# Accumulating eight projection blocks behind each norm by input chunk, and ordering the first loads to match

## The reference, cut to what matters

```python
cond = jax.nn.silu(c)
for l in range(DEPTH):
    mod = cond @ ada_w[l] + ada_b[l]                 # 6 x 1024 values: shift, scale, gate, twice
    sh1, sc1, g1, sh2, sc2, g2 = jnp.split(mod, 6, axis=-1)
    h = rmsnorm(x, norm1_g[l]) * (1.0 + sc1[:, None]) + sh1[:, None]
    x = x + g1[:, None] * token_mixer(h, positions, w_in[l], ...)   # proj = h @ w_in, 6656 columns
    h = rmsnorm(x, norm2_g[l]) * (1.0 + sc2[:, None]) + sh2[:, None]
    x = x + g2[:, None] * peer(h, peer_wq[l], ...)                  # q = h @ wq, 2048 columns
return rmsnorm(x, final_g)
```

## Time and profile before

| | |
|---|---|
| median of 3 runs | 2004.83 us (2003.58 to 2005.3) |
| span of the profiled execution, first to last instruction | 2001.2 us |
| median less span | 3.6 us |
| PE / PEld busy | 1945.8 / 1854.1 us |
| DVE / ACT / POOL busy | 1710.9 / 1240.9 / 441.9 us |
| mean granted clock of PE | 0.991 |
| moved by DMA | 480.52 MB, mean 240 GB/s |

### The profile page before, as it was taken

One profiled execution on the slowest core, in us unless ns is written; L12 is line 12 of the kernel. 1 busy time (PEld: TensorE's weight loads), 2 busy tenths in 40 slices (PEclk: granted clock), 3 DMA queues, 4 the chain that ended last, 5 costly groups with the idle time before them and its releaser, 6 DMA issues.

```text
span 2001.2 us, 39536 instructions
## 1 busy us (share of the span) xinstructions
PE 1945.8 (97%) x14478; PEld 1854.1 (93%) x14478; DVE 1710.9 (85%) x3168; ACT 1240.9 (62%) x2387; POOL 441.9 (22%) x312
## 2 busy tenths in 40 slices
PE   6999999999999999999989998999999999999998
PEld 6899899999999999999978898999999999999997
DVE  7876988999799888888788878899988888888887
ACT  3478545666888655555555775566668885555554
POOL 0000000000556433344100000000016543443440
PEclk7999999999999999999999999999999999999999
DMA  8764755666666799988767557555665558999884
GB/s 334 276 238 149 262 191 171 200 199 203 212 214 208 251 319 324 321 322 322 257 229 249 206 173 248 197 190 197 200 210 169 165 163 289 323 319 321 323 321 139
DMA packets 133554, 480.52 MB, mean 240 GB/s; under 512 B 16048, under 2 KB 16688, under 8 KB 132784
## 3 DMA queue, kind: packets, MB, share of 16 engines
q1 hardware_dynamic: 114992, 411.74, 60.6%
q0 software_dynamic: 18432, 67.12, 8.9%
HBM read 473.61 MB, written 1.57 MB: 237 GB/s over the span
## 4 chain that ended last, share of the span: by engine, by line
PE 87%; DVE 6%; ACT 3%; issue 2%; DMA 2%; SPq 0%; POOL 0%; DVEq 0%; ACTq 0%
PE ps L1777 20%; PE ps L1773 12%; PE ps L1474 11%; PE ps L1416 9%; PE ps L1412 8%; PE ps L1413 8%; PE ps L1478 6%; PE ps L1409 2%; PE ps L1746 2%; PE ps L1518 2%; ACT w_hi L564 2%; DVE w_lo L865 1%; DMA raw<-in_win 1%; PE ps L1464 1%; PE ps L1705 1%
## 5 line engine op out<-in xcount | busy, mean ns | idle before, releaser
L865 DVE TENSOR_TENSOR w_lo<-raw,w_hi 128x1024 fp32r<-128x1024 f32 x664 | 812.0, 1223 | 164.3 <-ACT w_hi L564 161.6
L564 ACT CAST w_hi<-raw 128x1024 fp32r<-128x1024 f32 x664 | 695.1, 1047 | 395.7 <-PE ps L1416 204.5
L1777 PE MATMUL ps<-p_both,w_hi 128*128 128x448 f32 x1952 | 440.1, 367 | 1.0 <-DVE p_both L1255 1.0
L1412 PE MATMUL ps<-h_both,w_hi 128*128 128x224 f32 (+1 forms) x1640 | 393.9, 282 | 2.5 <-ACT big L569 1.2
L1413 PE MATMUL ps<-h_both,w_hi 128*128 128x224 f32 (+1 forms) x1640 | 386.4, 278 | 0.0
L1777 PEld LDWEIGHTS ps<-p_both,w_hi 128*128 128x128 f32 x1952 | 349.3, 189 | 24.5 <-issue 1.3
L540 POOL TENSOR_SCALAR hot<-con,rt 128x128 f32<-128x128 f32 x168 | 198.1, 1190 | 640.0 <-DVE neg L1330 528.4
L1412 PEld LDWEIGHTS ps<-h_both,w_hi 128*128 128x128 f32 x1640 | 314.1, 192 | 5.5 <-issue 3.3
L1413 PEld LDWEIGHTS ps<-h_both,w_hi 128*128 128x128 f32 x1640 | 314.6, 192 | 0.0
L792 ACT CAST p_both<-big 128x224 fp32r (+1 forms) x256 | 97.0, 380 | 303.5 <-PE ps L1773 303.5
L1773 PEld LDWEIGHTS ps<-p_both,w_lo 128*128 128x128 f32 x2048 | 269.2, 191 | 7.6
(11 more groups left out here) (214 smaller groups left out, 2363.9 us busy)
## 6 DMA issues: line engine op xcount, KB each, us to landing
raw<-in_u SPq DMA_DIRECT2D x256, 512.0 KB, 3.5
raw<-in_v SPq DMA_DIRECT2D x256, 512.0 KB, 5.5
raw<-in_win SPq DMA_DIRECT2D x104, 512.0 KB, 4.4
hot<-in_ada SPq DMA_DIRECT2D x60, 512.0 KB, 4.9
big<-in_ada SPq DMA_DIRECT2D x36, 512.0 KB, 6.3
raw<-in_wq SPq DMA_DIRECT2D x32, 512.0 KB, 4.6
raw<-in_wout SPq DMA_DIRECT2D x16, 512.0 KB, 4.0
big<-in_decay SPq DMA_DIRECT2D x2, 1536.0 KB, 12.6
```

Of the source, the lines that this page charges most:

```text
L564: nc.scalar.copy(w_hi[:, j % 2, :], raw[:, j, :]).then_inc(hi_ready, 1)
L865: tt(w_lo[:, j % 2, :], raw[:, j, :], w_hi[:, j % 2, :].bitcast(F32), ALU.subtract).then_inc(lo_ready, 1)
L1412: mm(o, w, h_hi[:, k, 0:nd], start=(k == 0), stop=False)
L1777: return mm(bank(YC[c])[:, 0:2 * nd].rearrange("p (a t) -> p a t", a=2), w_hi[:, s, P * c:P * (c + 1)], p_both[:, s, :, 0:nd], start=begin ...
```

## The change

- `project_pair` is gone. `project_eight` makes blocks 0 to 7 together: for each of the eight input chunks k it runs eight matmuls w_hi by h_hi, eight w_hi by h_lo, eight w_lo by h_hi, one for each block, into PSUM banks 4 to 7. The first eight blocks of `w_in` and of `wq` are laid out for it by input chunk, so chunk k needs weight block k alone. One ACT routine, `take_eight`, copies all four banks out when all is done. The wide form is no longer used for blocks 2 to 7 of layer 1, and `project_v` no longer waits for copies.
- At the program's start the loads are issued by chunk: constants, positions, c, x, vectors, then modulation blocks and weight blocks alternately, eight weight blocks instead of four. `first_scales` run on PE after chunks 2 and 4. DVE makes the first rotation table before anything else and the second behind the norm; the large decay table is loaded behind block 9.
- The work tied to steps moves: rotation to steps 9 to 12, retention two steps later, `MOD_AT` to a new table, the early units of the retrieval selection to steps 9 to 15.
- One of two DVE instructions in `gains` goes (the factor is put into the vectors once).

```diff
-MOD_AT = (5, 7, 9, 11, 12, 13, 14, 16, 18, 19, 21, 23, 25, 27, 42, 43, 47, 49, 51, 52, 53, 54, 55, 56,
-          B_WQ + 1, B_WQ + 2, B_WQ + 3, B_WQ + 4, B_WQ + 5, B_WQ + 6)
+MOD_AT = (14, 15, 16, 18, 21, 23, 25, 27, 37, 39, 41, 42, 43, 44, 45, 47, 49, 51, 52, 53, 54, 55, 56, 57,
+          B_WQ + 2, B_WQ + 3, B_WQ + 4, B_WQ + 5, B_WQ + 6, B_WQ + 7)
...
-Q_FIRST = 7
-N_EARLY = N_WQ - Q_FIRST
+UNITS_AT = {9: 1, 10: 1, 11: 2, 12: 1, 13: 2, 14: 1, 15: 1}
+N_EARLY = sum(UNITS_AT.values())
...
+            sp.dma_start(con[:], consts).then_inc(small_in, 16)
+            sp.dma_start(turned_at[:, 0, :].bitcast(I32), positions.partition_broadcast(P)).then_inc(pos_in, 16)
             sp.dma_start(cond[:], c.partition_broadcast(P)).then_inc(c_in, 16)
+            sp.dma_start(xT[:], x).then_inc(x_in, 16)
             sp.dma_start(vec[:], vectors).then_inc(vec_in, 16)
...
             for which in range(2):
                 mods_first(0, which)
-            mods_first(2, 1)
+            win_first(0)
+            win_first(1)
             for which in range(2):
                 mods_first(1, which)
-            win_first(0)
+            win_first(2)
+            mods_first(2, 1)
+            win_first(3)
+            mods_first(2, 0)
+            win_first(4)
             mods_first(3, 1)
...
+            win_first(5)
+            mods_first(3, 0)
+            for j in (6, 7):
                 win_first(j)
...
                 for k in range(KC):
+                    if q == 0 and k % 2 == 0:
+                        round_hi(k, k % RING)
                     act.wait_ge(scaled_x, KC * q + k + 1)
...
+                    if q == 0 and k % 2:
+                        round_hi(k, k % RING)
+                    if q == 0 and k == 1:
+                        turn_angles(0)
...
+            def take_eight(n, dst):
+
+                act.wait_ge(block_done, n + KC)
+                for a in range(KC // 2):
+                    nc.scalar.copy(dst[:, 2 * a:2 * a + 2, :], bank(4 + a).rearrange("p (a t) -> p a t", a=2)).then_inc(out_taken, 2)
...
                 for k in range(KC):
-                    if q == 0 and k in (0, 4, 6):
-                        for g in ((0, 1) if k == 0 else (k // 2,)):
-                            first_mods(g)
+                    if q == 0 and k % 2 == 0:
+                        first_mods(k // 2)
                         if k == 0:
                             rstd_chain(q)
-                            low(0, 0)
                     scale(k).then_inc(scaled_x, 1)
-                    if k:
+                    if q == 0 and k % 2:
+                        for a in (k - 1, k):
+                            h_low(q, sh, a)
+                            low(a, a % RING)
...
-                h_low(q, sh, KC - 1)
+                if q:
+                    h_low(q, sh, KC - 1)
+                else:
+                    for half in range(2):
+                        angle(1, half)
...
+            def project_eight(q, n):
+
                 for k in range(KC):
+                    s = k % 2
+
+                    def part(m, w, h):
+                        return mm(bank(4 + m // 2)[:, SEQ * (m % 2):SEQ * (m % 2 + 1)], w[:, s, P * m:P * (m + 1)], h[:, k, :],
+                                  start=(k == 0 and m % 2 == 0 and w is w_hi and h is h_hi),
+                                  stop=(k == KC - 1 and w is w_lo), skip_group_check=True)
+                    pe.wait_ge(hi_ready, n + k + 1)
                     pe.wait_ge(hhi_ready, KC * q + k + 1)
+                    for m in range(KC):
+                        part(m, w_hi, h_hi)
+                    pe.wait_ge(h_ready, KC * q + k + 1)
+                    for m in range(KC):
+                        part(m, w_hi, h_lo)
+                    pe.wait_ge(lo_ready, n + k + 1)
+                    for m in range(KC):
+                        last = part(m, w_lo, h_hi)
+                    last.then_inc(block_done, 1)
+                    if q == 0 and k in (2, 4):
+                        first_scales(PE_GROUP + (k - 2) // 2)
```

More of the change, by code:

```diff
@@ L763, in _ @@
                     round_hi(n + 2, (m + 2) % RING)
-                    take(n, qt[:, m:m + 1, :], ACT.Copy, m)
-                    if m in (6, 10, 14):
-                        copy_scores((m - 6) // 4)
+                    if m == KC - 1:
+                        take_eight(l * N_BLOCKS + B_WQ, qt[:, 0:KC, :])
+                    if m >= KC:
+                        take(n, qt[:, m:m + 1, :], ACT.Copy, m)
+                    if m in (8, 12, 14):
+                        copy_scores((8, 12, 14).index(m))
                 def fill(g):
@@ L943, in first_mods, with both @@
                                                    mod_sum[:, at + j:at + j + 1]).then_inc(mod_used, MOD_GROUP // mine)
-                if g == 0:
-                    dve.wait_ge(vec_in, 16)
                 dve.wait_ge(mod_used, MOD_GROUP * (g + 1))
-                for which, first in enumerate((SH1, SC1)):
-                    n = first + 2 * g
-                    made = mod_sum[:, at + 2 * which:at + 2 * which + 2]
-                    if which and by_pe:
-                        dve.wait_ge(scale_made, g - PE_GROUP + 1)
-                        made = bank(4 + g - PE_GROUP)[:, 0:2]
-                    st.link(tt(mod[:, 0, n:n + 2], made, vec[:, V_ADAB + n:V_ADAB + n + 2], ALU.add))
+                def both(row, first):
+                    return row[:, first:first + 2 * KC].rearrange("p (w k) -> p w k", w=2)[:, 0:mine // 2, 2 * g:2 * g + 2]
+                st.done(tt(both(mod[:, 0, :], SH1), mod_sum[:, at:at + mine].rearrange("p (w k) -> p w k", k=2),
+                           both(vec, V_ADAB + SH1), ALU.add))
+                if by_pe:
+                    n = SC1 + 2 * g
+                    dve.wait_ge(scale_made, g - PE_GROUP + 1)
+                    st.done(tt(mod[:, 0, n:n + 2], bank(2 + g - PE_GROUP)[:, 0:2], vec[:, V_ADAB + n:V_ADAB + n + 2], ALU.add))
+                st.wait()
                 gains(0, V_N1, SC1, 2 * g, 2 * g + 2)
@@ L1205, in _ @@
                 nc.vector.tensor_copy(ident_r, ident).then_inc(ident_ready, 1)
+                early = 0
                 for m in range(1, N_WQ):
@@ L1208, in _ @@
                     mod_at(B_WQ + m)
-                    if m >= Q_FIRST:
-                        unit((m - Q_FIRST) // UNIT_BLOCKS, (m - Q_FIRST) % UNIT_BLOCKS)
+                    for _ in range(UNITS_AT.get(m, 0)):
+                        unit(early // UNIT_BLOCKS, early % UNIT_BLOCKS)
+                        early += 1
                 n0 = l * N_BLOCKS + B_U
@@ L1403, in project @@
                 pe.wait_ge(hi_ready, n + 1)
-                ge(pe, out_taken, e - behind + 1)
+                if e is not None:
+                    ge(pe, out_taken, e - behind + 1)
                 o = bank(E[s])[:, 0:nd]
@@ L1505, in _ @@
                 square_sum(0, k)
-            first_scales(2)
-            first_scales(3)
             for l in range(DEPTH):
-                project_pair(2 * l, l * N_BLOCKS, l * EV)
+                project_eight(2 * l, l * N_BLOCKS)
                 def project_v(m):
@@ L1635, in att_sum @@
                     last.then_inc(att_out, 1)
-                for m in range(2, N_WIN):
+                for m in range(KC, N_WIN):
                     if C_RV <= m < C_AQ:
@@ L1694, in _ @@
                 square_sums(2 * l + 1)
-                project_pair(2 * l + 1, l * N_BLOCKS + B_WQ, l * EV + E_WQ)
+                project_eight(2 * l + 1, l * N_BLOCKS + B_WQ)
                 def scores(pair):
@@ L1707, in scores @@
                         last.then_inc(score_ready, 1)
-                for m in range(2, N_WQ):
-                    project(l * N_BLOCKS + B_WQ + m, l * EV + E_WQ + m, m % RING)
-                    if m in (5, 9, 13):
-                        scores((m - 5) // 4)
+                for m in range(KC, N_WQ):
+                    project(l * N_BLOCKS + B_WQ + m, l * EV + E_WQ + m if m >= KC + 2 else None, m % RING)
+                    if m in (8, 11, 13):
+                        scores((8, 11, 13).index(m))
                 for m in range(2):
@@ L1892 @@
     win = blocks(arr["w_in"][:, :, order])
+    win[:, :KC] = arr["w_in"][:, :, order[:D]].reshape(DEPTH, KC, P, D)
+    wq = blocks(arr["peer_wq"])
+    wq[:, :KC] = arr["peer_wq"][:, :, :D].reshape(DEPTH, KC, P, D)
     rv, av = (arr["w_in"][:, :, at[n]] for n in ("rv", "av"))
```

142 lines of the change are left out of this document (59 added, 83 removed).

## The result

The changed kernel takes 2022.25 us in the median of 4 runs (2019.92 to 2023.13), the kernel before in the same session 2005.07 (2003.58 to 2006.05): a ratio of 1.0084 (95% interval 1.0072 to 1.0097), slower by 0.84%. The medians differ by 17.2 us. The profiled spans, 2021.0 us against 2001.2, differ by 19.8: the profiled execution of the changed kernel was a little slower than its median and that of the kernel before a little faster, so some 2.6 us of what the two traces show is the difference between executions. The forecast was 2007.3, with a range from 1995 to 2011.

A forecast was written before the change was run, and what follows sets the result against it. PE was taken as the bound (87% of the chain of waits). On the 2001.2 us span, -5.1 + 5.8 - 0.65 - 3.2 + 6.5 - 0.9 = +2.5 gave 2003.7; with 3.6 to the median 2007.3, range 1995 to 2011.

The forecast's parts named there:

- The stalls at step 57: End of w_out, both layers: DVE waits for a late product row, PE idles 4.5 and 5.2 us; costs 5.8 and 6.5.
- Rival A: End of w_out: the product of step 57 doesn't hold PE up, both costs go; 1995.0 us, chance 0.22.
- Nothing for both, at worst 1 us: w_in steps 9 to 12 and early units: DVE falls 1.3 us behind, less than a low's 1.7 lead; no cost.
- The start: Program start to first value block: 7.8 us gained by earlier chunks, 2.7 lost to the clock; 5.1 won.
- the forecast value block: First value block after the start: begins at 54.5 us by the step count, before the clock's loss of 2.7.
- The groups: Start: two groups of first_scales on PE, counted at 4.13 us each.
- The clock: Start: one slow stretch of 3.1 us behind each of two first_scales groups, 2.7 us lost together.
- rival B: Start: first_scales groups at 0.50, slow chunks behind; 6.9 us more, 2014.2; sign over 7 us at 0.50; chance 0.14.
- Rival D: Start: loads of eight weight blocks delay modulation blocks, so blocks reach PE no sooner; 2012 us, chance 0.04.
- The norms: Eight-block stretches behind norms 1, 2 and 3: won 0.65, 3.2 and 0.9 us; 24.6 us at norm 1.

The follow-up runs named there:

- the second execution: The changed kernel run and profiled once more, unaltered: 2018.78 us, 1.0066 of the kernel before.
- The last version: Changed kernel with product step 57 replaced by 19, rotations reordered, only scale group 3 on PE (behind chunk 3), vectors loaded ahead of x: 1990.6 us, 0.9932.
- the three edits: Changed kernel with product step 57 replaced by 19, retention rotations reordered, scale products behind chunks 1 and 3: 1993.95 us, 0.9944.
- the four versions built on these edits: The three edits plus vectors ahead of x, one scale group on PE, none, or one and vectors: 1993.73, 1992.56, 1993.63, 1990.6 us.

## Why the prediction was wrong

**The stalls at step 57: right.** Forecast 5.8 and 6.5 us; PE stood 4.25 and 4.14 us, DVE waited 2.7 us for the row, its product began 8.05 us after the row's issue, and without it the stages are 5.2 and 5.9 us shorter (4.6 and 4.1 against the second execution). Taking the entry out of the changed kernel and putting it into the kernel before say the same. Rival A falls.

**The step that failed most: "Nothing for both, at worst 1 us",** on `w_in` steps 9 to 12. It measured 10.0 us by the stages of the first execution and 7.5 by those of the second; the stall in PE that it left out is 3.35 to 5.07 us in layer 0 and 1.7 to 2.1 in layer 1 in six executions, with slow matmuls behind it. The working counted what the rotations cost DVE (1.9 us a step) and left out the transfers they wait for. Before, the four swaps lay two blocks apart and DVE never waited for one, in either layer. Moved together, the third can be issued only after the first rotation (at 71.01), and what it takes then (3.2 us of issuing, 5.0 of landing) is longer than the two steps of DVE's work that lay between (to 75.0). For the modulation rows the working followed the queue; for the swaps it did not. The new order of the rotations with fewer to wait for takes PE's stall away, as the experiment showed.

**The start: -0.3 in place of -5.1.** From the forecast value block (54.5 + 2.7 = 57.2) to the real one (61.93) are 4.7 us. Chunk 2 began at 30.94 and not at 28.5: 1.3 of it because the squares waited for the vectors longer than counted (11.53, not 10.2), 1.1 because the sums took 6.48 and not 5.42. The groups took 4.11 and 3.50 from start to next start in place of 4.13 each: -0.65. The clock is the rest, and the term of the start's sum that was mis-sized most: six chunks lose 5.6 us and not 2.7. There were three slow stretches rather than two, since one follows the pause ahead of chunk 2 as well. The sign named for rival B came too: the mean of 0.73 over the 19 us from 31 to 50 makes about 10 us at 0.50, more than the 7 it asked for. But only half of its mechanism did: slow chunks, while the groups ran at full rate or fell only in their last part, 2.9 us where it had 6.9. Rival D falls: DVE's products for chunks 2 and 3 begin at 24.68 with no wait for a row. The -0.3 itself is uncertain by some 1.5 us either way, by when the first load landed: where the start's program is the same, the first matmul came at 8.84 and 10.34 before the change, and at 12.07 and 13.21 after it. DVE's waits of 3.20 and 1.59 us for the scale products cost nothing directly: PE was never idle meanwhile. The last version takes 8.6 us less than the changed kernel in this stage, so the start can pay.

**The norms: about right.** Where neither stall is (the three edits) the stages differ from before by +0.3, +0.2, -2.8 and -0.8, against 0, -0.65, -3.2 and -0.9. Only the third is clear of the spread; in the four versions built on these edits it is -3.4 to -4.2. The eight blocks of norm 1 took 25.8 us, from 264.16 to 289.96, and not 24.6:

```profile
264.16 3.75 PE L1476 MATMUL ps<-h_both,w_hi 128*128 128x256 f32 x16 [3.09 <-ACT h_both L616]
...
269.42 2.47 PE L1476 MATMUL ps<-h_both,w_hi 128*128 128x256 f32 x16
```

The slow stretch reaches into the second chunk there, 1.2 us more of loss than the forecast took from the row of `project_pair`.

**The sum.** On the span: 2003.7 forecast, + 10.0 for the swaps, + 4.8 for the start, + 1.7 for the norms, - 1.2 for step 57 gives 2019.0, where 2021.0 was measured. The missing 2 us are no more than what one stage differs between executions of one program (1.8 us to norm 3 in the changed kernel), and where they belong is open. On the medians the miss is 15.0 us, since the median lay 1.25 us above the profiled span and not 3.6: the forecast had added a difference that hangs on which execution was profiled. The range was too narrow on the side where the move of many steps at once could hide another wait like the one that was found.

## What to carry to other kernels

When steps of an engine's schedule are drawn together, list for each the transfer it waits for, when that can first be issued (free buffer, source ready, queue position), and its landing time; here waits of 2.7 and 4.2 us on DVE, which works in the order of its program, made PE stand 4.25 and 5.07 us, each with a slow stretch behind it. Before giving up a restructuring that loses, cut both traces at common landmarks: the new structure, with its scale products moved, left the span 7 us shorter, nearly all of it at the start and at norm 2, and one entry of a table and the order and the waits of four rotations hid it. What the structure is worth without the new order of loads wasn't tried. An engine that was made earlier only wins if what it needs next is early too: of the 2.8 us by which chunk 0 came sooner 0.9 was left at the value block.

## What the runs showed of the hardware

- The clock's level isn't fixed by the program alone. At norm 2 two executions of the changed kernel, behind the same pause of 3.09 us, took 3.53 us for sixteen matmuls (granted clock 0.54 over the 3.36 us of this chunk's w_hi part) and 2.14 (1.00). The first, then the second:

```profile
1031.77 3.53 PE L1476 MATMUL ps<-h_both,w_hi 128*128 128x256 f32 x16 [3.09 <-ACT h_both L616]
```

```profile
1031.12 2.14 PE L1476 MATMUL ps<-h_both,w_hi 128*128 128x256 f32 x16 [3.09 <-ACT h_both L616]
```

- A group of scale products (x32 in the rows) takes 3.63 us at the upper level, 6.99 at the lower, and 4.0 to 5.5 where the level changes within it; in every profile with such a group a chunk that is slow in part or whole follows the last one, even where dense matmuls ran right up to the group (47.76, then 51.26, in the changed kernel).
- With the swaps' small transfers among the loads, the DMA engines are busy without moving much: between 76 and 82 us of the changed kernel their busy share was 0.99 at 233 GB/s, where with 512 KB loads alone it is 1.03 at 410 (31.0 to 34.5). From 67.0 to 69.3, when SP issued nothing but swap pieces, it was 0.47 at 127.

```profile
76.00:82.00 6.00, 0.93 (x6) 0.57 (x6) 2.69 (x4) 1.33 (x2) 0.00 (x0) 0.76 0.99 233
```
